# First input piece of the mixers and the convolution multiplied by token half, 128 moving columns in place of 256

## The chip, the core and the metric

One NeuronCore of a Trainium2 chip. The metric is the device time of one execution in microseconds. The kernel before was timed three times: 3643.92, 3650.49 and 3654.88 us.

## What is computed

A stack of transformer-like layers over 256 tokens of width 1024, in fp32. Four layers of the first block, each `ffn, mixer, ffn`, with the mixers gated delta rule (layers 0 and 3), stick-breaking attention (1) and sparse latent attention (2); then two layers of a second block, one with attention over a context and one with a gated convolution. Cut to what matters here:

```python
for i in range(4):
    x = x + 0.5 * swiglu(rmsnorm(x, ffn1_norm[i]), ffn1_w_gu[i], ffn1_w_down[i])
    h = rmsnorm(x, mix_norm[i])
    x = x + (gated_deltanet, stick_breaking_attention, dsa_sparse_attention)[i % 3](h, ...)   # starts with h @ w_in
    x = x + 0.5 * swiglu(rmsnorm(x, ffn2_norm[i]), ffn2_w_gu[i], ffn2_w_down[i])
...
xn = modulate(x, norm_g[1, 1], m[3], m[4])
bg, cg, h = jnp.split(xn @ w_in, 3, axis=-1)      # conv_mixer
```

## The kernel before

**Tiling.** The 256 tokens are two halves `t` of 128. All weights come as pieces of 128 x 2048 fp32 (1 MB), numbered `ns` in the order of use, in three slots (`SLOTS`). SyncE loads a piece into `raw` once `lo_ready` says that the slot's last piece is split; ScalarE rounds it to `w_hi` once TensorE has used the slot (`w_used`); VectorE writes `w_lo = raw - w_hi` (line 1861) and raises `lo_ready`. Activations are split in the same way into `h_hi` and `h_lo`. A product is three single-pass matmuls: high by high, high by low, low by high (`products`, lines 558 to 562). The format is fp32r; a plain fp32 matmul (those on `const`, `arena`, `der`) takes several passes and leaves two records in the trace for each matmul.

**A projection.** `across` (line 564) multiplies a piece of 256 output channels: for each of 8 groups `q` of input channels and two halves `b` of the output, three matmuls with 128 x 128 weights held in the array and all 256 tokens moving, 48 in all. The result lies in one PSUM bank, output half `b` in columns 256 b to 256 b + 255.

**The opening of a mixer or of the convolution.** The stage before it has updated `x` half by half. ScalarE's `statistics` gives the norm's factor of a token half, VectorE's `normalise` (line 1910) writes `h` for that half and raises `xn_ready`; TensorE transposes it in `turn(i, t, half)` (line 593), four 128 x 128 transposes for four channel groups, into bank `2 t + half` of `acc`; ScalarE writes `h_hi` (`turned_high`), VectorE `h_lo` (`turned_low`, lines 1889 and 1892) and raises `n_lo_ready`. The transposes of token half 0 are already issued at the end of the stage before, so `turn_all` (line 618) issues those of token half 1 alone. VectorE's own order in `opening` (line 2050) is: low part of (token half 0, groups 0 to 3), normalise token half 1, low part of (0, groups 4 to 7), (1, groups 0 to 3), (1, groups 4 to 7), then the splits of the next two weight pieces. ScalarE's is alike. `turned_bank(i, t, half)` is the count of `n_lo_ready` at which (t, half) is ready.

In before, the first piece is `across(ns, ..., n_at=...)`: group 0 waits for (1, groups 0 to 3), group 4 for (1, groups 4 to 7), since every matmul moves both token halves. The stages touched are `gdn` (mix_0 and mix_3), `sb` (mix_1), `dsa` (mix_2) and `conv` (b1_conv), five openings in an execution. The convolution has 16 small plain fp32 matmul passes, `gate_rows` (line 631), ahead of its transposes of token half 1. The stage `attn` and the feed-forward stages are not touched.

Of the kernel before, what the change touches and what calls it, by code (L numbers as in the profile page):

```python
# [14 lines left out]
P = 128  # L15
T = 256
D = 1024
KC = D // P
F = 2816
STEPS = F // 256  # L20
SLOTS = 3
# [260 lines left out]
def build(nc, wts, vec_d, const_d, x_d, c_d, bias_d, mods_d, rows_d, out, ops):  # L282
    starts, use, total = schedule(ops)

    with ExitStack() as ctx:
# [98 lines left out]
        w_used = sem("w_used")  # L384
# [34 lines left out]
        def before(i, what):  # L419

            if what == "h":
                return sum(H_SPLIT[k] for k, _, _ in ops[:i])
            if what == "h_written":
                return sum(H_WRITTEN[k] for k, _, _ in ops[:i])
            if what == "norm":
                return sum(norms(k) for k, _, _ in ops[:i])
            if what == "turn":
                return sum(TURNS[k] for k, _, _ in ops[:i])
            if what == "xn":
                return 2 * sum(TURNS[k] for k, _, p in ops[:i] if not late(k, p))  # L430
            if what == "acc":
                return sum(ACC_FULL[k] for k, _, _ in ops[:i])
            if what == "ffn":
                return sum(k == "ffn" for k, _, _ in ops[:i])
            if what == "x":
                return 4 * sum(k in UPDATES and p.get("x") == "x" for k, _, p in ops[:i])
            if what == "c":
                return 4 * sum(k in UPDATES and p.get("x") == "c" for k, _, p in ops[:i])
            if what == "side":
                return 16 * sum(k == "gdn" for k, _, _ in ops[:i]) + 3 * sum(k == "sb" for k, _, _ in ops[:i])  # L440
            if what == "gdn_ops":
                return sum(k == "gdn" for k, _, _ in ops[:i])
            if what in PIECES:
                return sum(k == what for k, _, _ in ops[:i])
            raise KeyError(what)
# [28 lines left out]
        def turned_bank(i, t, half, nth=0):  # L474

            return 4 * (before(i, "turn") + nth) + 2 * t + half + 1

        def tok(t):
            return slice(t * P, (t + 1) * P)
# [71 lines left out]
        def _(pe):  # L551
            def bank(u):

                if u >= BANKS:
                    pe.wait_ge(taken, u - BANKS + 1)
                return wrk[:, u % BANKS, :]

            def products(o, l_h, l_l, r_h, r_l, first, last):

                nc.tensor.matmul(o, l_h, r_h, start=first, stop=False, skip_group_check=True)  # L560
                nc.tensor.matmul(o, l_h, r_l, start=False, stop=False, skip_group_check=True)  # L561
                return nc.tensor.matmul(o, l_l, r_h, start=False, stop=last, skip_group_check=True)  # L562

            def across(ns, o, h_at=None, n_at=None, kc=KC, inside=None):

                pe.wait_ge(lo_ready, ns + 1)
                s = ns % SLOTS
                for q in range(kc):
                    if inside and q == 3:
                        inside()  # L570
                    if h_at is not None:
                        pe.wait_ge(h_lo_ready, h_at + q + 1)
                    if n_at is not None and q % 4 == 0:
                        pe.wait_ge(n_lo_ready, n_at + 3 + q // 4)
                    for b in range(2):
                        c0 = q * 256 + b * P
                        m = products(o[:, b * T:(b + 1) * T], w_hi[:, s, c0:c0 + P], w_lo[:, s, c0:c0 + P],
                                     h_hi[:, q, :], h_lo[:, q, :], q == 0 and b == 0, q == kc - 1)
                return m.then_inc(w_used, 1)
# [13 lines left out]
            def turn(i, t, half, nth=0, src=None):  # L593
# [21 lines left out]
                    m = nc.tensor.transpose(o[:, b * P:(b + 1) * P], v[:, t, k * P:(k + 1) * P], cst("ident"))  # L615
                m.then_inc(turned, 1)

            def turn_all(i, nth=0):
                for t in range(2):
                    for half in range(2):  # L620
                        turn(i, t, half, nth)
# [164 lines left out]
            def gdn(i, name, prm):  # L786
# [22 lines left out]
                    for u in units:  # L809
                        side(u // 2, u % 2)  # L810

                turn_all(i)
                across(ns, put("gates"), n_at=4 * before(i, "turn"))
                sides(range(12))
                pe.wait_ge(stage("gdn_gates"), g + 1)
                o = put("cols")
# [147 lines left out]
            def sb(i, name, prm):  # L964
                ns, h0, e = starts[i]["ns"], before(i, "h"), HEADS * before(i, "sb")
                put = lambda label: bank(use[name, label])
                mm = nc.tensor.matmul
                a0 = before(i, "side")

                def side(u):  # L970

                    f, part = u // 2, u % 2
                    pe.wait_ge(lo_ready, ns + 9 + f + 1)
                    o, s = acc[:, f, :], (ns + 9 + f) % SLOTS
                    for q in range(4 * part, 4 * part + 4):
                        for t in range(2):
                            w = slice(q * 256, (q + 1) * 256)
                            m = products(o[:, t * 256:(t + 1) * 256], h_hi[:, q, tok(t)], h_lo[:, q, tok(t)],
                                         w_hi[:, s, w], w_lo[:, s, w], q == 0 and t == 0, q == KC - 1)
                    if part:  # L980
                        m.then_inc(w_used, 1)

                def out_piece(j):

                    pair, n, t = j // 4, j // 2 % 2, j % 2
                    m = out_part(i, ns + 12, h0, n, t, wait=True, qs=range(2 * pair, 2 * pair + 2))
                    if pair and t:
                        m.then_inc(w_used, 1)

                def logits(n):  # L990

                    o = put(f"z{n}")
                    mm(o[:, 0:T], s_k[:, n, 0:P], s_q[:, n, :], start=True, stop=True)
                    mm(o[:, T:T + P], s_k[:, n, P:T], s_q[:, n, P:T], start=True, stop=True).then_inc(filled, 1)

                turn_all(i)
                for p in range(8):
                    across(ns + p, put(f"qk{p}"), n_at=4 * before(i, "turn") if p == 0 else None)
                pe.wait_ge(taken, use[name, "qk7"] + 1)
                along(ns + 8, put("v0"))  # L1000
                logits(0)
                for n in range(HEADS + 2):
                    if n + 1 < HEADS:
                        logits(n + 1)
                    for u in SB_SIDE.get(n, []):
                        side(u)
                    if n < HEADS:
                        o, sp = put(f"s{n}"), s_sp[:, n % 2, :]
                        pe.wait_ge(stage("sb_sp"), e + n + 1)
                        mm(o[:, T:T + P], cst("suffix"), sp[:, T:T + P], start=True, stop=True)  # L1010
                        mm(o[:, 0:T], cst("suffix"), sp[:, 0:T], start=True, stop=False, skip_group_check=True)
                        mm(o[:, P:T], cst("ones"), sp[:, T:T + P], start=False, stop=True, skip_group_check=True).then_inc(filled, 1)
                    if n >= 2:
                        k = n - 2
                        pe.wait_ge(stage("sb_att"), e + k + 1)
                        if k % 2 == 0:
                            if k:
                                pe.wait_ge(side_taken, a0 + k // 2)
                            else:
                                pe.wait_ge(taken, use[name, "v0"] + 1)  # L1020
                        weigh_values(put(f"o{k}"), s_v, k, s_att[:, k % 4, :]).then_inc(filled, 1)
                    if n == min(SB_PARTS):
                        pe.wait_ge(side_taken, a0 + 3)
                    for j in SB_PARTS.get(n, []):
                        out_piece(j)
                out_second(i, ns + 12, h0)

            def dsa(i, name, prm):
# [49 lines left out]
                        m.then_inc(w_used, 1)  # L1078

                q_side, kv_side = (c_hi, c_lo), (h_hi, h_lo)  # L1080
                turn_all(i)
                across(ns, put("p0"), n_at=4 * before(i, "turn"))
                across(ns + 1, put("p1"))
                across(ns + 2, put("p2"), inside=query_norms)
                grouped(3, 3, 512, 0, "qi0", q_side, False, h_at=h0)
# [159 lines left out]
            def conv(i, name, prm):  # L1245
                ns, h0 = starts[i]["ns"], before(i, "h")
                gate_rows(i, name, prm)
                turn_all(i)
                for p in range(4):
                    for k, n in enumerate(("cg", "hh", "bg")):  # L1250
                        across(ns + 3 * p + k, bank(use[name, f"{n}{p}"]), n_at=4 * before(i, "turn") if p == k == 0 else None)
                out_proj(i, ns + 12, h0)

            pe.wait_ge(loaded, 16 * LOADS)
# [1683 lines left out]
```

## Time and profile before

| | |
|---|---|
| median of three runs | 3650.49 us |
| the profiled execution | 3655.45 us, its span 3653.7 us |
| TensorE (PE) busy | 3502.4 us, 96% |
| VectorE (DVE), ScalarE (ACT) busy | 2212.2 us, 1713.6 us |
| TensorE's mean granted clock | 0.979 |
| DMA | 654.62 MB, mean 179 GB/s |

PE is a matmul record, PEld the load of the 128 x 128 operand that is held in the array; such a load overlaps matmuls. A matmul's record is longer than its place in the queue (0.28 us at starts 0.12 us apart), since matmuls are pipelined; so prices are taken from distances of starts. PEclk is the granted TensorE clock: 1.00 is 2.4 GHz, 0.50 is 1.2 GHz. In a matmul's name the moving operand stands first, then the held one.

### The profile page before, as it was taken

How to read it: one execution, taken by the hardware profiler on the slowest of the kernel's cores; microseconds unless marked ns; L12 is line 12 of the kernel's file. 1: busy time of each engine (PE TensorE's matmuls, PEld its weight loads, DVE VectorE, ACT ScalarE, POOL GpSimd, SP SyncE). 2: the span in 40 equal slices, each digit the busy share in tenths (PEclk: the TensorE clock that was granted, in tenths of full speed). 3: DMA queues.
4: the chain of work that ended last, by engine and by line, in shares of the span. 5: the costliest groups of instructions: out<-in, count | busy, mean ns of one | idle time of the engine just before them, and what ended most of it. 6: DMA issues, size and time to landing. Idle time of an engine off the chain costs nothing. (4 is left out here: it accounts for less than half of the span.)

```text
span 3653.7 us, 44766 instructions
## 1 busy us (share of the span) xinstructions
PE 3502.4 (96%) x18386; PEld 2975.5 (81%) x18386; DVE 2212.2 (61%) x2602; ACT 1713.6 (47%) x2072; POOL 113.8 (3%) x116
## 2 busy tenths in 40 slices
PE   8999899999999998999999899999998899999999
PEld 7889778888888877788888878888888678788887
DVE  5776557666567677576677555555455554545554
ACT  5453354544544445545454444545453444544443
POOL 0001100000000000000001100000000000000000
PEclk9999899999999998999999999999999999999999
DMA  6632146564377663576742145455543135454353
GB/s 265 242 139 81 47 182 233 214 238 164 133 254 269 255 235 121 198 282 240 276 173 93 58 160 186 179 190 182 186 174 139 58 138 183 172 186 160 147 206 127
DMA packets 90409, 654.62 MB, mean 179 GB/s; under 512 B 10080, under 2 KB 10208, under 8 KB 11360
## 3 DMA queue, kind: packets, MB, share of 16 engines
q1 hardware_dynamic: 79200, 574.15, 42.8%
q0 software_dynamic: 11008, 77.60, 5.8%
q8 instruction: 149, 2.44, 0.3%
q14 instruction: 52, 0.43, 0.0%
HBM read 650.66 MB, written 1.05 MB: 178 GB/s over the span
## 5 line engine op out<-in xcount | busy, mean ns | idle before, releaser
L1861 DVE TENSOR_TENSOR w_lo<-raw,w_hi 128x2048 fp32r<-128x2048 f32 x541 | 1236.6, 2290 | 642.8 <-ACT w_hi L1268 642.6
L1268 ACT ACTIVATE w_hi<-raw 128x2048 fp32r<-128x2048 f32 x541 | 1032.2, 1912 | 505.7 <-PE acc L562 394.7
L560 PE MATMUL wrk<-w_hi,h_hi 128*128 128x512 f32 (+1 forms) x2416 | 945.9, 392 | 18.8 <-issue 10.8
L562 PE MATMUL wrk<-w_hi,h_lo 128*128 128x512 f32 (+1 forms) x2416 | 930.4, 385 | 0.0
L561 PE MATMUL wrk<-w_lo,h_hi 128*128 128x512 f32 (+1 forms) x2416 | 928.5, 384 | 0.0
L560 PEld LDWEIGHTS wrk<-w_hi,h_hi 128*128 128x128 f32 x2416 | 455.9, 189 | 106.9 <-issue 13.6
L562 PEld LDWEIGHTS wrk<-w_hi,h_lo 128*128 128x128 f32 x2416 | 455.3, 188 | 91.5
L561 PEld LDWEIGHTS wrk<-w_lo,h_hi 128*128 128x128 f32 x2416 | 456.3, 189 | 85.5 <-issue 0.7
L560 PE MATMUL acc<-w_hi,hid_hi 128*128 128x512 f32 x1144 | 448.0, 392 | 4.7 <-DVE hid_lo L1953 4.5
L562 PE MATMUL acc<-w_hi,hid_lo 128*128 128x512 f32 x1144 | 445.5, 389 | 0.0
L561 PE MATMUL acc<-w_lo,hid_hi 128*128 128x512 f32 x1144 | 445.1, 389 | 0.0
L1268 ACT ACTIVATE hid_hi<-wrk 128x512 fp32r<-128x512 f32 x143 | 85.8, 600 | 461.6 <-PE wrk L659 461.6
L1268 ACT ACTIVATE arena<-wrk 128x512 f32<-128x512 f32 (+2 forms) x276 | 136.5, 496 | 326.6 <-PE wrk L562 181.9
L560 PEld LDWEIGHTS acc<-w_hi,hid_hi 128*128 128x128 f32 x1144 | 214.8, 188 | 51.0 <-issue 7.4
L562 PEld LDWEIGHTS acc<-w_hi,hid_lo 128*128 128x128 f32 x1144 | 214.7, 188 | 44.7
L561 PEld LDWEIGHTS acc<-w_lo,hid_hi 128*128 128x128 f32 x1144 | 214.9, 188 | 43.7
L1953 DVE TENSOR_TENSOR hid_lo<-wrk,hid_hi 128x512 fp32r<-128x512 f32 x143 | 98.7, 690 | 248.9 <-ACT hid_hi L1268 248.9
L1921 DVE SCALAR_TENSOR_TENSOR arena<-arena,c 128x1024 f32<-128x1024 f32 x184 | 217.3, 1219 | 0.0
L560 PE MATMUL wrk<-h_hi,w_hi 128*128 128x256 f32 x560 | 166.4, 297 | 20.8 <-DVE h_lo L1892 12.0
L1268 ACT ACTIVATE arena<-wrk,stat 128x256 f32<-128x256 f32 x176 | 83.8, 477 | 209.6 <-PE wrk L562 209.5
L560 PE MATMUL acc<-h_hi,w_hi 128*128 128x256 f32 x576 | 170.7, 296 | 9.4 <-DVE w_lo L1861 9.0
L561 PE MATMUL acc<-h_lo,w_hi 128*128 128x256 f32 x576 | 165.6, 288 | 0.0
(274 smaller groups left out, 3991.0 us busy)
## 6 DMA issues: line engine op xcount, KB each, us to landing
raw<-in_wts SPq DMA_DIRECT2D x541, 1024.0 KB, 4.8
arena<-in_mods POOLq DMA_DIRECT2D x72, 1024.0 KB, 5.1
const<-in_const SPq DMA_DIRECT2D x1, 2112.0 KB, 16.7
c<-in_bias POOLq DMA_DIRECT2D x8, 256.0 KB, 2.9
x<-in_x SPq DMA_DIRECT2D x2, 512.0 KB, 6.4
c<-in_c SPq DMA_DIRECT2D x1, 1024.0 KB, 4.8
out<-x SPq DMA_DIRECT2D x1, 1024.0 KB, 3.9
row<-in_rows SPq DMA_DIRECT2D x1, 512.0 KB, 17.4
```

The source lines that it names most:

```text
L560: nc.tensor.matmul(o, l_h, r_h, start=first, stop=False, skip_group_check=True)
L561: nc.tensor.matmul(o, l_h, r_l, start=False, stop=False, skip_group_check=True)
L562: return nc.tensor.matmul(o, l_l, r_h, start=False, stop=last, skip_group_check=True)
L1268: return nc.scalar.activation(o, i, f, **kw)
L1861: tt(w_lo[:, ns % SLOTS, :], raw[:, ns % SLOTS, :], w_hi[:, ns % SLOTS, :].bitcast(F32), ALU.subtract).then_inc(lo_ready, 1)
L1921: ins = stt(m_prod[:, b, 0:D], m_raw[:, m % 2, b * D:(b + 1) * D], 1.0, m_rows[:, w, :], ALU.mult, ALU.mult, accum_out=der[:, l, w, j:j + 1])
L1953: tt(hid_lo[:, s % 2, :, :], wrk[:, use[name, f"t{s}"] % BANKS, :].rearrange("p (a b) -> p a b", b=T), hid_hi[:, s % 2, :, :].bitcast(F32) ...
```

## The change

`across_by_half` takes the place of `turn_all` and the first `across` in the four stage functions. It waits for the weights, transposes what is left of token half 0 (nothing, as a rule), multiplies token half 0 by groups 0 to 3 once that part's low part is there, transposes token half 1, and multiplies the other three parts, each with its own wait. Each matmul moves one token half, 128 columns, so there are 4 parts of 24 matmuls, 96 in all. The argument `put(...)`, which waits for a free bank, is now evaluated ahead of the transposes of token half 1. In `sb` and `conv` the loop over the other pieces skips the first.

```diff
+            def across_by_half(i, ns, o):
+
+                pe.wait_ge(lo_ready, ns + 1)
+                s = ns % SLOTS
+
+                def part(t, half):
+                    pe.wait_ge(n_lo_ready, turned_bank(i, t, half))
+                    for q in range(4 * half, 4 * half + 4):
+                        for b in range(2):
+                            c0 = q * 256 + b * P
+                            m = products(o[:, b * T + t * P:b * T + (t + 1) * P], w_hi[:, s, c0:c0 + P], w_lo[:, s, c0:c0 + P],
+                                         h_hi[:, q, tok(t)], h_lo[:, q, tok(t)], t == q == b == 0, q == KC - 1)
+                    return m
+
+                turn(i, 0, 0)
+                turn(i, 0, 1)
+                part(0, 0)
+                turn(i, 1, 0)
+                turn(i, 1, 1)
+                part(0, 1)
+                part(1, 0)
+                return part(1, 1).then_inc(w_used, 1)
...
-                turn_all(i)
-                across(ns, put("gates"), n_at=4 * before(i, "turn"))
+                across_by_half(i, ns, put("gates"))
...
-                turn_all(i)
-                for p in range(8):
-                    across(ns + p, put(f"qk{p}"), n_at=4 * before(i, "turn") if p == 0 else None)
+                across_by_half(i, ns, put("qk0"))
+                for p in range(1, 8):
+                    across(ns + p, put(f"qk{p}"))
...
-                turn_all(i)
-                across(ns, put("p0"), n_at=4 * before(i, "turn"))
+                across_by_half(i, ns, put("p0"))
...
-                turn_all(i)
+                across_by_half(i, ns, bank(use[name, "cg0"]))
                 for p in range(4):
                     for k, n in enumerate(("cg", "hh", "bg")):
-                        across(ns + 3 * p + k, bank(use[name, f"{n}{p}"]), n_at=4 * before(i, "turn") if p == k == 0 else None)
+                        if p or k:
+                            across(ns + 3 * p + k, bank(use[name, f"{n}{p}"]))
```

## Rows read from the trace of the kernel before

**Rows 1.** The page: busy time by engine, and the clock in 40 slices.
```profile
PE 3502.4 (96%) x18386; PEld 2975.5 (81%) x18386; DVE 2212.2 (61%) x2602; ACT 1713.6 (47%) x2072; POOL 113.8 (3%) x116
...
PEclk9999899999999998999999999999999999999999
```

**Rows 2.** Stretches: limits, length, busy time of PE, PEld, DVE, ACT, POOL, PEclk, DMA.
```profile
3359.50:3421.00 61.50, 61.50 (x515) 61.50 (x514) 34.19 (x41) 24.48 (x18) 0.00 (x0) 1.00 0.45 171
```

**Rows 3.** Timeline, opening of mix_2: start, duration, engine, line, [idle before <- releaser].
```profile
1362.27 1.03 PE L615 MATMUL acc<-const,h 128*128 128x128 f32 x8
...
1364.15 1.13 DVE L1889 SCALAR_TENSOR_TENSOR h_lo<-acc,vec,h_hi 128x128 fp32r<-128x128 f32 x4 [1.00 <-ACT h_hi L1268]
...
1366.39 1.54 PE L615 MATMUL acc<-const,h 128*128 128x128 f32 x8 [3.09 <-DVE h L1910]
...
1368.29 2.16 DVE L1889 SCALAR_TENSOR_TENSOR h_lo<-acc,vec,h_hi 128x128 fp32r<-128x128 f32 x8 [0.56 <-ACT h_hi L1268]
...
1369.57 0.55 PE L560 MATMUL wrk<-h_hi,w_hi 128*128 128x256 f32 x1 [1.63 <-DVE h_lo L1889]
...
1370.37 4.49 DVE L1861 TENSOR_TENSOR w_lo<-raw,w_hi 128x2048 fp32r<-128x2048 f32 x2
...
1377.22 0.28 PE L560 MATMUL wrk<-h_hi,w_hi 128*128 128x256 f32 x1
...
1377.34 0.28 PE L561 MATMUL wrk<-h_lo,w_hi 128*128 128x256 f32 x1
```

**Rows 4.** Stretches around the five first pieces, columns as in rows 2.
```profile
210.00:213.00 3.00, 1.06 (x8) 0.86 (x8) 1.89 (x6) 2.42 (x10) 0.00 (x0) 1.00 0.00 0
213.00:214.20 1.20, 0.00 (x0) 0.00 (x0) 1.20 (x5) 1.20 (x5) 0.00 (x0) 0.57 0.03 7
214.20:219.90 5.70, 5.64 (x26) 5.67 (x27) 5.35 (x6) 1.59 (x1) 0.00 (x0) 0.50 0.24 68
...
863.60:868.50 4.90, 4.86 (x23) 4.89 (x24) 4.90 (x6) 1.57 (x1) 0.00 (x0) 0.50 0.18 37
...
1365.30:1366.80 1.50, 0.41 (x4) 0.41 (x5) 0.94 (x2) 1.25 (x6) 0.00 (x0) 1.00 0.00 0
1367.00:1369.50 2.50, 0.93 (x5) 0.53 (x3) 1.95 (x8) 2.38 (x9) 0.00 (x0) 0.50 0.00 0
1369.50:1373.70 4.20, 4.13 (x19) 4.17 (x20) 4.20 (x6) 1.59 (x1) 0.00 (x0) 0.50 0.07 16
...
1874.40:1878.80 4.40, 4.38 (x20) 4.40 (x21) 4.40 (x6) 1.54 (x1) 0.00 (x0) 0.50 0.12 15
...
3342.80:3345.50 2.70, 1.95 (x18) 1.76 (x16) 1.71 (x3) 2.67 (x6) 0.00 (x0) 1.00 0.00 0
...
3351.20:3356.80 5.60, 5.57 (x26) 5.60 (x27) 4.35 (x3) 4.07 (x6) 0.00 (x0) 0.50 0.08 20
```

**Rows 5.** Timeline, the first low part in the two other kinds of opening (mix_0, convolution).
```profile
208.85 1.13 DVE L1889 SCALAR_TENSOR_TENSOR h_lo<-acc,vec,h_hi 128x128 fp32r<-128x128 f32 x4 [1.03 <-ACT h_hi L1268]
...
3344.77 0.69 DVE L1892 TENSOR_TENSOR h_lo<-arena,h_hi 128x512 fp32r<-128x512 f32 x1 [0.92 <-ACT h_hi L1268]
```

**Rows 6.** Prices: 32 passes in the timeline; loads: ns min/median/max, or count, us, mean ns.
```profile
316.34 3.79 PE L887 MATMUL wrk<-arena 128*128 128x128 f32 x32
...
L560 PEld LDWEIGHTS wrk<-w_hi,h_hi 128*128 128x128 f32 x2416 | 455.9, 189 | 106.9 <-issue 13.6 <-DVE w_lo L1861 8.8 <-DVE arena L2285 1.0
...
L1237 PEld LDWEIGHTS wrk<-arena x88: 132/137/230, 2901.3 to 2941.9; 128*64 128x64 f32 x88
...
L615 PEld LDWEIGHTS acc<-const,h x192: 137/140/226, 206.7 to 3459.6; 128*128 128x128 f32 x192
```

**Rows 7.** Low clock elsewhere: stretches, and one group of matmuls in the second.
```profile
2957.80:2960.80 3.00, 3.00 (x7) 2.41 (x8) 0.96 (x2) 2.61 (x7) 0.00 (x0) 0.50 0.00 0
...
384.90:397.40 12.50, 12.50 (x48) 11.07 (x49) 5.79 (x9) 0.77 (x1) 0.00 (x0) 0.50 0.00 0
...
L826 PE MATMUL wrk<-arena,const 40*128 40x256 f32 x8 | 3.8, 651 | 0.0
```

## The prediction

> **What bounds the kernel now.** I read the page first, then the timeline of one changed opening, then stretches of all five, then the prices. The page [rows 1]: TensorE is busy 96% of the span at a clock of 0.9 or more, so what matters is time that the change adds to TensorE's queue or takes from it. After each opening TensorE runs on without a gap: 61.50 of 61.50 us behind the convolution's [rows 2], and the same view shows no gap of a microsecond for at least 24 us behind the four others. Whatever the first piece ends earlier or later, everything behind it moves by that amount; ScalarE and VectorE, which split later weights, wait for TensorE's slots and move along.
>
> The opening of mix_2 [rows 3]. The reader is to see a ladder. The transposes of half 0 run at 1362.27. VectorE has the low part of (half 0, channels 0 to 3) at 1364.15 + 1.13 = 1365.28, and nobody uses it. TensorE idles 3.09 us, transposes half 1 at 1366.39, idles 1.63 us, and starts the piece at 1369.57. It also starts at the lower clock level: the stretches of the five first pieces show a granted clock of 0.50, that is 1.2 GHz [rows 4]. There one 256-column matmul takes 4.90 / 23 = 0.213 us; at 2.4 GHz the starts are 1377.22 and 1377.34, so 0.120 us [rows 3]. One piece is 8 x 2 x 3 = 48 matmuls.
>
> How long is that from "first low part ready" (plus 0.15 us until TensorE moves, as between 1369.4, the middle of the eight low operations at 1368.29, and 1369.57) to the end of the piece? The end is the end of the stretch at 0.50 plus the matmuls left at 0.120. mix_0: low part 208.85 + 1.13 = 209.98, so start 210.1; end 219.9 + 22 x 0.12 = 222.5: 12.4 us. mix_1, with the same row at 858.26: 859.5 to 868.5 + 25 x 0.12 = 871.5: 12.0. mix_2: 1365.4 to 1373.7 + 29 x 0.12 = 1377.2: 11.8. mix_3, the row at 1869.04: 1870.3 to 1878.8 + 28 x 0.12 = 1882.2: 11.9. Convolution: 3344.77 + 0.69 + 0.15 = 3345.6 to 3356.8 + 22 x 0.12 = 3359.4: 13.8 [rows 3 to 5]. Together 61.9 us. That is the budget that the new order must beat.
>
> **Part one, the number of matmuls.** The 48 of 256 columns become 96 of 128. The columns streamed are the same, the weight loads double: 96 in place of 48. No row shows a single-pass matmul of 128 moving columns, so I bound it. Lower end: half of the 256-column time, 0.060 us. Upper end: 0.227 us, two passes of a plain fp32 matmul of 128 columns; 32 such passes take 3.79 us, so (3.79 - 0.275) / 31 = 0.113 each [rows 6], and the code issues 16 matmuls for them. The nearest row is that one pass, since it has the same weight load. And the load is the limit: for these operands it takes 189 ns with 128 columns and 137 with 64, so 0.8 ns a column, or 102 ns for 128 beside a fixed part that overlaps [rows 6]. The transposes' loads of 128 columns take only 140. [...] I take 0.114 at 2.4 GHz and 0.213 at 1.2 GHz (102 ns doubled, and the row of 0.213 has the same load).
>
> The Trainium skill (TensorE: Matmul & The Clock Gate, "LDWEIGHTS (loading the stationary operand)") gives about 107 ns for 128 columns, which the 102 from the rows agrees with. Its section "Back-to-back issue gap" gives about 81 ns for a stream of loads and matmuls at N = 128; by that the piece would be 96 x 0.081 = 7.8 us, which speaks for the cheap rival below; no row here shows such a spacing with 4-byte weights.
>
> **Part two, the order.** TensorE may start 4.2 us earlier (1365.4 in place of 1369.6). The transposes of half 1 now stand behind the 24 matmuls of part(0, 0): 1365.4 + 24 x 0.114 = 1368.2 at the high clock, in place of 1366.4, a slip of 1.8 us. Behind them wait ScalarE's h_hi and VectorE's h_lo of half 1 (end 1370.45, then 1372.3), and behind those the weight split of the next piece (1370.37 + 2.24 = 1372.6, then 1374.5). All of it is covered by part(0, 1) and part(1, 0), which need only half 0 and the first quarter of half 1; the cover is gone only if matmuls cost under about 0.08 us. SyncE's loads hang on lo_ready and slip with it, under a queue three pieces deep. The wait on lo_ready now stands ahead of the transposes, and so does the bank's; both were fulfilled long before (the first weight's low part is written before the opening, the bank's previous user is four uses back). These cost nothing.
>
> At the high clock throughout, an opening is then 96 x 0.114 = 10.9, plus 8 transposes at 0.11 = 0.9, plus 0.2 for the first matmul after the idle time: 12.0 us. Five: 60 us against 61.9. **The earlier start is paid back by the doubled loads**: -2 us, and +1 with 0.120 a matmul. Without the clock the change is worth nothing.
>
> **Part three, the clock.** In before, the clock went to 0.50 during or behind the idle time: it is 1.00 from 210.0 to 213.0 and 0.57 in the next 1.2 us; 1.00 up to 1366.8 and 0.50 from 1367.0 [rows 4], and in mix_1 and mix_3 it falls near 861.7 and 1872.0 in the same view. The new order still has 2.1 us with no instruction on TensorE after the first transposes, and then matmuls in which the array streams only half of the time (53 of 114 ns). I expect the fall at about the same moments in the four mixers. What brings the clock back? From 2957.8 TensorE ran three microseconds of full 512-column matmuls at 0.50 and was back. But from 384.9 to 397.4 the records show it busy for 12.50 of 12.50 us and the clock at 0.50 all along; 8 of its 48 records are matmuls on 40 partitions, 3.8 us [rows 7]. So a queue without a gap did not bring it back there. The new stream is one in which the array rests half of the time because of the loads; I think that it is nearer to the second stretch than to the first, and that the clock stays at 1.2 GHz to the end of the piece.
>
> The Trainium skill (same page, "What's actually happening") says that the clock follows how busy the engine was; with busy taken as a full queue that is rival 1, and [rows 7] speak against that reading.
>
> The sum for a mixer at 1.2 GHz: 96 x 0.213 = 20.5, 8 transposes 1.7, start 0.2: 22.4 us. Each microsecond before the fall does 0.213 / 0.114 = 1.87 us of this work, which takes 0.87 off. From the start to the fall it is about 3.1, 2.2, 1.5 and 1.7 us, so 19.7, 20.5, 21.1 and 20.9 us: 82.2 against 48.1, +34.1. Then the next piece of 256 columns brings the clock back as before's first pieces did, in 4.2 to 5.7 us; I take 4.5, each at a loss of 0.093 / 0.213: 4 x 2.0 = +8. The convolution has its gate-row matmuls right ahead (TensorE busy 1.95 of 2.70 us, [rows 4]) and now no long idle time behind them, so it stays at 2.4 GHz: 12.0 against 13.8, -1.8. Total 34.1 + 8 - 1.8 = +40 us. The profiled execution took 3655.45 us (span 3653.7), 5 above the median of 3650.49; the difference goes on the median: **3691 us**.
>
> **The rivals.**
> 1. The clock holds or returns during the piece. For it: the queue has no gap once it has begun, and the idle time shrinks from 4.7 to 2.1 us. With no fall -2 us; with the same low stretches as before (24.5 us, each losing 1 - 0.114 / 0.213 = 0.465), +9. Time 3648 to 3660: no change.
> 2. The cheap matmul, on the other side: loads hide, 0.06 to 0.08 us each. The bound becomes the next piece's low part: in mix_2 the transposes slip by only 0.5 us, the split ends at 1373.2 and the next piece starts there, 4.0 us earlier; five give -20, or about -5 to -10 where the clock falls. Time about 3633: faster. It decides where the load costs less than 0.08 us. Against it: 189 and 137 ns, and no pass under 0.11 anywhere.
> 3. Below 256 columns the single-pass format runs at the plain fp32 rate: 96 x 0.227 = 21.8, plus 1.1: 22.9 against 12.4 in each opening, +52, with the array fully used and the clock high. Time 3703. For it: nothing in the trace uses the format below 256 columns, so nothing excludes it.
> 4. That the parts don't interleave as said: part(0, 0) waits only for turned_bank(i, 0, 0), which VectorE writes before it normalises half 1. Nothing speaks for this.
>
> **How the numbers follow.** Forecast 0.43; rival 1 0.30; rival 3 0.12; rival 2 0.09; other small losses of 10 to 30 us (the clock stays low in one or two openings only) 0.06. A measurement of this kernel can tell about 0.3%, 11 us. Faster 0.10, same 0.32, slower 0.58. Rival 1 and the forecast both belong in the range, so 3642 to 3706. The forecast's own range is 3680 (one opening spared) to 3702 (the convolution falls too).
>
> **What would show it.** In the timeline: the first 128-column matmul 0.15 us after the first h_lo, near 4.2 us earlier than before (else rival 4); two starts 0.11 to 0.12 us apart where the clock is 1.00 and 0.21 where it is 0.50 (0.06 to 0.08: rival 2; 0.22 at a clock of 1.00: rival 3). In the stretches by clock: 0.50 from the second part of the first piece into the second piece in the four mixers, and 1.00 in the convolution; a clock of 1.00 over most of the piece is rival 1. Span of the first pieces 20 to 21 us in the mixers. The prediction is wrong if the clock counts a queue full of loads as work, or if a load does not take what the two durations say.

## The result: slower by 0.46%, less than half of what was forecast

| | median of 11 runs | lowest to highest |
|---|---|---|
| before | 3654.88 us | 3643.92 to 3659.21 |
| changed | 3669.34 us | 3662.11 to 3679.90 |

The ratio is 1.0046, with a 95% interval of 1.0036 to 1.0055. The forecast was +40 us, the change cost about 15. The profiled execution of the changed kernel took 3670.61 us, its span is 3668.7.

The page of the changed kernel, its busy time and clock, which answers to [rows 1]:

```profile
PE 3526.6 (96%) x18626; PEld 3003.1 (82%) x18626; DVE 2213.2 (60%) x2602; ACT 1713.5 (47%) x2072; POOL 113.5 (3%) x116
...
PEclk9999999999999998999989999999999999999999
```

TensorE has 240 records more (18386 before), the 5 x 48 additional matmuls, and is busy 24 us longer. Nothing else has changed in amount. The timeline of mix_2's opening answers to [rows 3]; columns: start, duration, engine, line, and in brackets the idle time before it and its releaser.

```profile
1359.58 1.03 PE L615 MATMUL acc<-const,h 128*128 128x128 f32 x8
...
1361.47 1.13 DVE L1911 SCALAR_TENSOR_TENSOR h_lo<-acc,vec,h_hi 128x128 fp32r<-128x128 f32 x4 [1.00 <-ACT h_hi L1290]
...
1362.74 0.30 PE L560 MATMUL wrk<-h_hi,w_hi 128*128 128x128 f32 x1 [2.13 <-DVE h_lo L1911]
...
1363.10 0.28 PE L560 MATMUL wrk<-h_hi,w_hi 128*128 128x128 f32 x1
1363.21 0.27 PE L561 MATMUL wrk<-h_lo,w_hi 128*128 128x128 f32 x1
...
1365.19 0.41 PE L561 MATMUL wrk<-h_lo,w_hi 128*128 128x128 f32 x1
1365.40 0.41 PE L562 MATMUL wrk<-h_hi,w_lo 128*128 128x128 f32 x1
...
1366.26 1.93 PE L615 MATMUL acc<-const,h 128*128 128x128 f32 x8
...
1370.62 4.48 DVE L1883 TENSOR_TENSOR w_lo<-raw,w_hi 128x2048 fp32r<-128x2048 f32 x2
...
1383.02 0.41 PE L562 MATMUL wrk<-h_hi,w_lo 128*128 128x128 f32 x1
1383.23 0.52 PE L560 MATMUL wrk<-h_hi,w_hi 128*128 128x256 f32 x1
```

The reader is to see: the first narrow matmul starts 0.14 us behind the low part, 3.16 us behind the first transposes (7.30 in before). Starts lie 0.11 us apart, then, from 1364.56 on, 0.21. The transposes of half 1 begin at 1366.26. The next piece's split (the first of the two at 1370.62, 2.24 us each) ends at 1372.9, ten microseconds before TensorE wants it. The piece ends at 1383.23: 20.49 us, where before had 11.8 from the same point. Now the stretches by clock (columns as in [rows 2]), mix_2 first, then mix_1 and mix_0 of the same execution, which answer to [rows 4]:

```profile
1362.70:1364.50 1.80, 1.75 (x16) 1.79 (x17) 1.32 (x4) 1.20 (x5) 0.00 (x0) 1.00 0.00 0
...
1367.80:1383.20 15.40, 15.40 (x74) 15.40 (x73) 6.56 (x10) 3.54 (x8) 0.00 (x0) 0.50 0.36 136
1383.20:1388.40 5.20, 5.20 (x26) 5.20 (x26) 2.43 (x2) 2.43 (x2) 0.00 (x0) 0.50 0.00 0
1388.50:1400.00 11.50, 11.47 (x89) 11.09 (x89) 4.32 (x10) 4.93 (x8) 0.00 (x0) 1.00 0.25 93
...
860.10:868.10 8.00, 8.00 (x74) 8.00 (x73) 6.56 (x10) 3.79 (x9) 0.00 (x0) 1.00 0.16 56
...
210.90:217.60 6.70, 6.70 (x34) 6.70 (x34) 1.77 (x5) 1.73 (x8) 0.00 (x0) 0.50 0.00 0
217.70:225.50 7.80, 7.80 (x71) 7.80 (x72) 6.57 (x10) 3.04 (x6) 0.00 (x0) 1.00 0.26 87
```

Mix_2 is the forecast's picture: the clock falls during the first part, stays at 1.2 GHz for 15.40 us of a queue without a gap, and comes back 5.2 us into the next piece. Mix_1 never leaves 2.4 GHz. Mix_0 falls at once and comes back at 217.7, just behind its transposes. From first matmul to the next piece the five openings take 14.84 (mix_0), 11.59 (mix_1), 20.49 (mix_2), 21.06 (mix_3) and 13.22 us (convolution), 81.2 in all where before had 61.9 by the same reckoning, 19.3 more. The spans differ by only 15.0; the rest lies behind the openings, where no instruction was changed: the distance from mix_0's transposes to the next stage's is 3.5 us shorter than in before, although its opening is longer. Distances of that kind also differ between two profiles of one kernel: mix_3's whole stage takes 257.8 us in the first profile of before and 263.1 in the second (before_again).

### The profile page after: what moved, and what is told of

It is laid out like the page before. It is cut to its first block and busy times, and to the rows that moved or that the text cites. A ratio compares the mean times of both kernels' runs of the same rounds, so it can differ in the third digit from the quotient of the medians.

```text
span 3668.7 us, 45246 instructions
## 1 busy us (share of the span) xinstructions
PE 3526.6 (96%) x18626; PEld 3003.1 (82%) x18626; DVE 2213.2 (60%) x2602; ACT 1713.5 (47%) x2072; POOL 113.5 (3%) x116
## 5 line engine op out<-in xcount | busy, mean ns | idle before, releaser
L560 PE MATMUL wrk<-h_hi,w_hi 128*128 128x256 f32 (+1 forms) x640 | 192.5, 301 | 19.7 <-DVE h_lo L1914 9.8
L561 PE MATMUL wrk<-h_lo,w_hi 128*128 128x256 f32 (+1 forms) x640 | 191.6, 299 | 0.0
L562 PE MATMUL wrk<-h_hi,w_lo 128*128 128x256 f32 (+1 forms) x640 | 191.4, 299 | 0.0
```

## The experiments

Four theories of where the extra time comes from. A: a narrow matmul (128 moving columns) costs nearly what a wide one (256) does, and the clock, once at 1.2 GHz, does not come back while a stream of narrow ones runs. B: the clock comes back as in before, and the 48 additional matmuls with their loads alone cost. C: the new order and the waits that it moves cost. D, added later: which opening is long belongs to the stage.

### The width alone

```diff
-                turn(i, 0, 0)
-                turn(i, 0, 1)
-                part(0, 0)
-                turn(i, 1, 0)
-                turn(i, 1, 1)
-                part(0, 1)
-                part(1, 0)
+                turn_all(i)
+                pe.wait_ge(n_lo_ready, turned_bank(i, 1, 0))
+                part(0, 0)
+                part(1, 0)
+                part(0, 1)
```

> The order and the waits of the kernel before, only with 96 matmuls of 128 columns in place of 48 of 256 in the five first pieces. Theory A (the loads bound the stream, and the clock, once at 1.2 GHz, does not come back during it): in the kernel before all five pieces begin at the low clock, so nearly every piece here stays at it, 96 x 0.213 = 20.5 us in place of 7.6 to 8.4, and the next piece takes some 4 us more to bring the clock back: about +13 to +14 us for each opening, +55 to +70 in all, 3710 to 3720. Rival B (the clock comes back during the stream as it did in before): 5 us low (23 matmuls) and 73 at 0.112, so 13.1 us, +5 each, +25, 3678. Rival C (the extra time of the changed kernel came from the new order, not from the width): within 10 us of before.

Measured: 3716.68 us (3714.21 to 3726.78), ratio 1.0182 (1.0156 to 1.0209), +61 us by the medians. All five pieces take 20.54 us. Mix_2's piece and what follows:

```profile
1389.40:1409.90 20.50, 20.50 (x96) 20.50 (x97) 5.38 (x6) 1.62 (x1) 0.00 (x0) 0.50 0.27 103
1410.00:1414.00 4.00, 4.00 (x20) 4.00 (x20) 1.32 (x2) 2.43 (x2) 0.00 (x0) 0.50 0.00 0
1414.10:1430.00 15.90, 15.88 (x123) 15.39 (x123) 9.13 (x15) 7.30 (x10) 0.00 (x0) 1.00 0.24 72
```

96 narrow matmuls, 20.5 us at 0.50; then 256-column matmuls, and the clock is back 4 us later. B (+25) and C (within 10) fall. With the same 96 matmuls the old order costs 61 us and the new one 15.

### Twice the columns on the same loads

```diff
-                            m = products(o[:, b * T + t * P:b * T + (t + 1) * P], ...,
-                                         h_hi[:, q, tok(t)], h_lo[:, q, tok(t)], ...)
+                            m = products(o[:, b * T:(b + 1) * T], ...,
+                                         twice(h_hi[:, q, tok(t)]), twice(h_lo[:, q, tok(t)]), ...)
```

Here `twice` repeats a token half along a stride of zero. The first pieces then hold something else; loads, waits and order are those of the changed kernel.

> The changed kernel with each of the 96 matmuls of a first piece moving its token half twice, 256 columns (the two copies are added into both output halves, so the first pieces hold something else): twice the columns on the same loads, waits and order. Theory A: 0.213 us each at 1.2 GHz as with 128 columns, 0.120 at 2.4 in place of 0.112 (+0.8 us an opening), but the clock comes back within some 7 us, so no opening takes more than 16 us where the changed kernel took 20.5 and 21.0. Sum 3652 to 3664, faster than the changed kernel in spite of more work. Rival B (the extra time is the loads and slips alone): 96 x 0.008 x 5 = 4 us slower than the changed kernel, 3673. If the clock counts only the time in which the queue has work, the low stretches look like those of the changed kernel.

Measured: 3657.01 us (3651.53 to 3664.47), ratio 1.0013 (1.0000 to 1.0026). **Twice the columns, and 12 us less than the changed kernel.** The mixers take 13.95 to 13.97 us each, the convolution 12.44. Mix_0 with its transposes of half 1, then mix_2:

```profile
210.30:213.70 3.40, 3.40 (x16) 3.40 (x17) 1.88 (x5) 1.13 (x5) 0.00 (x0) 0.50 0.00 0
...
214.73 1.04 PE L615 MATMUL acc<-const,h 128*128 128x128 f32 x8
...
1364.10:1367.30 3.20, 3.20 (x17) 3.20 (x17) 0.72 (x3) 0.00 (x0) 0.00 (x0) 0.50 0.02 5
1367.40:1376.40 9.00, 9.00 (x78) 9.00 (x77) 6.56 (x10) 3.98 (x9) 0.00 (x0) 1.00 0.21 73
```

The clock still falls at the start in all four mixers of this profile, and is back 3.4 us later in each. In mix_0 it is back at 213.7, a microsecond before the transposes begin, so the wide stream brought it back without them. At 1.2 GHz a matmul takes 0.213 us with 128 columns and with 256.

### The idle time filled, changed kernel

```diff
+            def fill(o, s, n):
+
+                for _ in range(n):
+                    nc.tensor.matmul(o[:, 0:NB], w_hi[:, s, 0:P], w_hi[:, s, 0:NB], start=True, stop=True, skip_group_check=True)
...
                 turn(i, 0, 1)
+                fill(o, s, 3 if ops[i][0] == "conv" else 8)
                 part(0, 0)
```

> The changed kernel with 8 extra matmuls of 512 columns (3 in the convolution) in the idle time ahead of the first part, into the bank that the first part then overwrites. Theory A: the clock is at 2.4 GHz when the stream begins and stays there, so each opening takes 11.6 us as mix_1 did (60 us for five where before has 62): 3647 to 3655, about the kernel before. Rival C (order and slips cost the time): no change against the changed kernel, 3669, or slower by the fillers. If a stream of half-used array also lets the clock fall, one or two openings still take 20 us, 3660 to 3670.

Measured: 3655.90 us (3650.39 to 3658.68), ratio 1.0006 (0.9994 to 1.0017): the loss is gone. The fillers and the piece in mix_2:

```profile
1360.37 2.07 PE L621 MATMUL wrk<-w_hi 128*128 128x512 f32 x8
...
1362.70:1374.20 11.50, 11.50 (x104) 11.50 (x104) 8.44 (x15) 5.18 (x14) 0.00 (x0) 1.00 0.11 37
```

All four mixers take 11.62 or 11.63 us, the convolution 11.77, sum 58.3. With the idle time filled, the narrow stream keeps 2.4 GHz from end to end in all five openings (11.50 us here). That it merely begins at 2.4 GHz isn't enough: without the fillers mix_2's stream began at it and lost it 1.8 us later. The width-only kernel shows the other side: begun at 1.2 GHz, the stream stays there. The sum of 58.3 is 3.6 us under before's 61.9, and that gain doesn't show in the time: the interval of the ratio allows 2.2 us at most. Why is open.

### The idle time filled, kernel before

`turn_filled` takes the place of `turn_all` in the four stage functions; `fill` is the same as above.

```diff
+            def turn_filled(i, ns, o):
+
+                a, b = (8, 12) if ops[i][0] == "conv" else (12, 6)
+                pe.wait_ge(lo_ready, ns + 1)
+                fill(o, ns % SLOTS, a)
+                turn_all(i)
+                fill(o, ns % SLOTS, b)
+                return o
```

> The kernel before with extra matmuls of 512 columns in the idle time ahead of the transposes of token half 1 (12, in the convolution 8) and behind them (6, in the convolution 12). Theory A: the first pieces run at 2.4 GHz, 5.8 us in place of 7.6 to 8.4, so -2 to -2.6 us in each opening, -10 to -12 in all: about 3642, faster than both kernels. If the low clock of the openings were no cost to the end, no change.

> The kernel before with the extra matmuls in the idle time of the five openings, once more with more rounds. Expected from the first time (0.9978) and from the five pieces of 5.8 us in its profile: 0.997 to 0.998 of before, near 3644, if the gain of 11 us in the openings reaches the end; 1.000 if it was chance in other stages.

Measured: first 3645.51 us (3634.96 to 3657.04), ratio 0.9978 (0.9962 to 0.9994), with one profiled execution of 3655.1 us of span; then 3642.31 us (3634.14 to 3648.93), ratio 0.9968 (0.9955 to 0.9982). It beats both kernels. The first profile fell on the longest of its ten executions, so five short pieces don't make every execution short: it had 123 us of low clock in its span, the second profile 99. All five pieces take 5.81 to 5.84 us in both profiles; mix_2's of the second:

```profile
1358.30:1364.10 5.80, 5.76 (x48) 5.79 (x49) 5.33 (x6) 1.57 (x1) 0.00 (x0) 1.00 0.20 68
```

### The changed kernel and the one before, profiled again

> The changed kernel unaltered, for a second profile. Theory A: each of the four mixer openings takes one of three forms: about 11.6 us where the clock does not fall, about 14 to 16 where it falls and comes back through the transposes, 20 to 21 where it stays low. Which one it takes differs from execution to execution, since the moment of the fall does not move with the kernel. Expected 2 of 4 mixers at 20 to 21, and a time of about 3650 plus 9 for each of them. Rival D (the form belongs to the stage: mix_2 and mix_3 fall because of what they do before): the same two openings fall again.

> As changed_again_1: a third profile of the same kernel. Theory A: another choice of openings stays low, and the time follows their number. Rival D: mix_2 and mix_3 again.

> As changed_again_1: a fourth profile of the same kernel. Theory A: another choice of openings stays low, and the time follows their number. Rival D: mix_2 and mix_3 again.

> The kernel before unaltered, for a second profile. Theory A: its five first pieces use the array fully, so wherever the clock falls it is back within some 7 us; the pieces take 5.8 us (no fall) to 8.4 us, and nothing near 20. That is why its executions lie closer together than the changed kernel's.

Measured, in us from the first matmul to the next piece:

| profile | time | mix_0 | mix_1 | mix_2 | mix_3 | conv |
|---|---|---|---|---|---|---|
| changed, first | 3670.61 | 14.84 | 11.59 | 20.49 | 21.06 | 13.22 |
| changed_again_1 | 3672.96 | 11.59 | 20.52 | 14.85 | 14.85 | 11.72 |
| changed_again_2 | 3655.95 | 11.59 | 13.22 | 13.22 | 14.85 | 11.73 |
| changed_again_3 | 3684.04 | 22.13 | 20.94 | 21.14 | 14.84 | 11.72 |
| before_again | 3658.95 | 8.31 | 8.00 | 7.34 | 7.45 | 8.17 |

The same opening, mix_0, in the third and the fourth profile of the changed kernel:

```profile
210.60:222.20 11.60, 11.55 (x104) 11.58 (x105) 8.44 (x15) 5.15 (x14) 0.00 (x0) 1.00 0.14 42
...
210.60:232.60 22.00, 22.00 (x104) 22.00 (x105) 8.44 (x15) 4.99 (x13) 0.00 (x0) 0.50 0.25 96
```

The same 104 matmuls and transposes behind the same wait, once at 1.00 in 11.6 us and once at 0.50 in 22.0. D falls as it was put: mix_0, mix_1 and mix_2 each take three forms. (Mix_3 and the convolution repeat theirs in three profiles of four; whether a stage leans to a form, four profiles can't tell.) What differs is the moment of the fall against the first narrow matmul. In 16 mixer openings, all behind 2.12 to 2.16 us without a matmul, and four of the convolution:

| fall behind the first narrow matmul | openings | length |
|---|---|---|
| just before it (0.02 us) | 1 | 22.1 |
| 0.18 to 1.02 us | 5 | 14.8 |
| 1.08 to 1.81 us | 5 | 20.5 to 21.1 |
| 1.94 to 2.33 us | 3 (one the convolution) | 13.2 |
| no fall | 6 (three the convolution) | 11.6 to 11.7 |

The groups don't overlap, and no fall came later than 2.33 us. The first narrow matmul of mix_0 stands at 210.3 to 210.7 us in all four profiles, and the clock fell once just before it, once 0.18 us behind it and twice not at all: the kernel's own timing doesn't set the moment.

The time does not follow the number of long openings alone: 3655.95 us with none, 3672.96 with one, 3670.61 with two, 3684.04 with three. The span less the five openings is 3587.5, 3597.7, 3589.5 and 3591.4 us in the table's order, and the low clock outside the openings' low stretches 79, 110, 88 and 93 us: the profile with one long opening lost its time elsewhere. The two long openings that were expected of each were met in none of the three.

### Half of the piece narrow

```diff
                 part(0, 0)
                 turn(i, 1, 0)
                 turn(i, 1, 1)
-                part(0, 1)
                 part(1, 0)
-                return part(1, 1).then_inc(w_used, 1)
+                pe.wait_ge(n_lo_ready, turned_bank(i, 1, 1))
+                for q in range(4, KC):
+                    ...  # the body of across: 24 matmuls of 256 columns
```

> The changed kernel with input groups 0 to 3 by token half (48 matmuls of 128 columns) and groups 4 to 7 as before (24 of 256): 72 loads in place of 96, and the last quarter of the piece uses the array fully. Theory A: where the clock does not fall, 2.7 + 0.9 + a wait for the first quarter of half 1 + 2.7 + 2.9, near 11 us; where it falls, 48 x 0.213 + 1.7 + 24 x 0.213 = 17 us at most, and the clock is back within 5 us behind the narrow matmuls. So the long openings of 20 to 21 us are gone: 3650 to 3660, at least 8 us under the changed kernel. Rival B (only the loads count, with the clock as in before): 24 loads less, 24 x 0.05 x 5 = 6 us under the changed kernel.

A miss: 3672.81 us (3666.25 to 3678.49), ratio 1.0059 (1.0040 to 1.0077), where 3650 to 3660 was expected. Mix_2's piece, from the fall of the clock to its return:

```profile
1368.20:1385.10 16.90, 15.36 (x72) 14.96 (x72) 8.23 (x15) 4.77 (x13) 0.00 (x0) 0.50 0.28 102
```

The stretch has a second idle time (16.90 - 15.36 = 1.54 us), since behind the transposes nothing is left to do until the first quarter of half 1 is there; it is 1.54 us in each mixer and 2.55 in the convolution. I had counted it in the fast case and not in the slow one. The clock fell in all five openings of this profile and came back in none before the wide matmuls: the openings take 18.2, 16.6, 18.2, 18.1 and 15.1 us. So none takes 20 us, and none 11 to 13. In the convolution the fall came behind the second idle time; in the mixers it came 0.3 to 1.1 us into the stream, before the missing part(0, 1) could matter. There the edit explains the new wait; whether it also explains that the clock came back late is argued from one profile and not shown. Fewer matmuls didn't make up for the lost cover.

## Why the prediction was wrong

**What bounds the kernel**: right. What an opening gained or lost came out at the end; from before to changed, the distances between the stages' transposes stay within 0.1 us in the feed-forward stages that lie between the mixers.

**The loads**: the price was right, its reason isn't shown. The price was taken as 0.114 us at 2.4 GHz and 0.213 at 1.2; it is 0.112 (starts from 217.80 to 225.39 in mix_0, 68 steps) and 0.213 (96 in 20.50). An undisturbed opening was put at 12.0 us, it takes 11.6. Rival 2 (0.06 to 0.08) and rival 3 (0.227) appear nowhere. The reason given was that the load is the limit, with 0.8 ns a column read from records of 189 and 137 ns. The rows don't bear that: the transposes' loads of 128 columns take 140 ns, as long as those of 64 columns ([rows 6]). And the plain pass that served as the nearest row costs the same with half the load. Eight of them with 64 columns held, in before:

```profile
2901.34 1.09 PE L1237 MATMUL wrk<-arena 128*64 128x128 f32 x8
```

That is (1.09 - 0.27) / 7 = 0.117 us each, against 0.113 with 128 columns held. So the load doesn't set the price of that pass. For the narrow single-pass matmul two readings stay open: the load bounds it, or 128 columns stream at half the rate of 256. Both fit what was measured, 0.112 against 0.120 us at 2.4 GHz and 0.213 for either width at 1.2. No run has the narrow matmuls with smaller loads, which would decide it; the sum needs the price alone. For a load of 128 columns the Trainium skill (TensorE: Matmul & The Clock Gate, "LDWEIGHTS (loading the stationary operand)") has a formula that gives about 107 ns, near the measured 0.112, which doesn't tell the two readings apart. The 81 ns that the Trainium skill gives for a stream at N = 128 (the same page, "Back-to-back issue gap") stands in no profile here.

**The order**: right in its parts. The first narrow matmul stands 4.14 us earlier against the transposes (3.16 in place of 7.30), the slips of half 1 and of the next piece's split are covered (split at 1372.9, wanted at 1383.2), the two waits put ahead cost nothing (the first narrow matmul starts 0.14 us behind its low part).

**The clock, its price**: right where it happened. Mix_2 and mix_3 were put at 21.1 and 20.9 us and took 20.49 and 21.06; the return was put at 4.5 us into the next piece, measured 5.2 and 4.0 (and 4.1 in mix_2 of the width-only kernel). From stage to stage they cost +11.2 and +9.9, put at +11.3 and +11.0. (Rival 1's 24.5 us of low stretches are 24.8 by [rows 4], which changes nothing in its sum.)

**The clock, how often**: here the prediction failed. The step was "I expect the fall at about the same moments in the four mixers", and with it "that the clock stays at 1.2 GHz to the end of the piece". The falls of before were carried over to the new order: in before they do repeat (all five openings in both profiles), in the new order they don't. The four profiles of the changed kernel have 16 mixer openings: 6 of 20.5 to 22.1 us, 5 of 14.8, 2 of 13.2 and 3 of 11.6. So the clock fell in 13 of the 16, and in 7 of those 13 it was back inside the piece. That return is a case that I hadn't: the clock comes back 0.45 to 2.1 us behind the start of the last of the eight transposes. These also stand inside the low stretch of the six long openings, so they go with a return but don't bring one each time. Of the difference to the forecast the returns make 2.7 us an opening and the missing falls 1.7. The mean of the 16 is 16.4 us, against the 20.5 of the forecast and against 12.0 before. By these four profiles, in place of "+34.1" stands 4 x 4.4 = 17.6 for the pieces, and in place of "+8" stands 3 behind them (1.5 long openings in an execution, some 2 us each); less 1.7 for the convolution (12.1 in the mean of four, 13.8 before). That makes +19; the interval of the measured ratio gives +13 to +20. Rival 1 (the clock holds or returns during the piece), given 0.30, was the other half of the truth, in 10 of 16 openings: which of the two happens changes from opening to opening and from execution to execution. A forecast of one or the other for all four was the mistake; a mean over openings was wanted.

**The convolution**: right. It was put at 12.0 us and takes 11.72 in three profiles and 13.22 in one, where the clock was low for 3.4 us.

## What to carry to other kernels

Halving the moving columns doubles the matmuls and the loads of the held operand; with 4-byte operands of 128 columns a matmul of 128 moving columns took 0.112 us and one of 256 took 0.120, so an earlier start must be worth more than 5 us for a piece of 48 matmuls before it pays. Look for what the clock does in the idle time that one wants to use: filling it with matmuls whose result is thrown away gave 0.2 to 0.3%, and rearranging the work to fill it gave nothing even where the clock held. Where a price depends on something that doesn't move with the kernel, as the moment at which the clock falls here, read it from several profiles and forecast the mean of the cases.

## What the runs showed that I had not expected

A queue full of narrow matmuls lost 2.4 GHz within its first 2.33 us or, in these profiles, not at all (8.00 us without a fall in mix_1, 11.50 in the filled kernel). But where no transposes stood in it, it never brought it back: it stayed low for 20.5 us in all five pieces of the width-only kernel. The same loads with 256 columns were back after 3.4 us, in mix_0 with no transposes inside that time; and before's own first pieces, with no transposes in them, 3.4 to 5.7 us behind their start in two profiles.

The varying openings hardly show in the spread of the times. The eleven executions of the changed kernel spread by 18 us (3662 to 3680), those of before, whose openings have no such forms, by 15 in eleven and by 17 in 25 (3643.82 to 3660.74). So the expectation that before's executions lie clearly closer together isn't borne out by these; only with the three further profiles does the changed kernel reach from 3655.95 to 3684.04 us.
